# Gated delta rule: chunk inverses kept on the other half of the rows, products in four corners of the array

## The reference, cut to what matters

```python
lower = where(strict, einsum('bhnid,bhnjd->bhnij', kb, k) * decay, 0.0)   # kb = k * beta
tmat  = lower + eye(c)
sol   = triangular_solve(tmat, rhs, lower=True, unit_diagonal=True)
# then a scan over the chunks:
v_new = u_i - w_i @ state
o_i   = qg_i @ state + qk_i @ v_new
state = state * gl_i + kg_i^T @ v_new
```

## Time and profile before

| | |
|---|---|
| three runs | 1930.01, 1932.18 (median), 1933.41 us |
| the profiled execution | 1931.5 us; first to last instruction 1929.7 us |
| mean granted TensorE clock | 0.963 of full |
| PE busy, weight loads busy | 91%, 73% |
| DVE, ACT, POOL busy | 43%, 37%, 31% |
| stage A, B, C in this execution | about 1175 to 1199 us, 1199 to 1278 us, 1278 to 1288 us |

### The profile page before, as it was taken

The page is one execution under the profiler, slowest core; times in us unless marked ns, Lnnn a source line. Parts: engine busy times, 40 slices in busy tenths (PEclk is TensorE's granted clock), DMA queues, the critical chain, the costliest instruction groups (busy, mean ns, idle before and its releaser), DMA issues.

```text
span 1929.7 us, 32336 instructions
## 1 busy us (share of the span) xinstructions
PE 1747.3 (91%) x13588; PEld 1403.6 (73%) x13588; DVE 824.2 (43%) x1489; ACT 716.7 (37%) x1111; POOL 601.3 (31%) x318
## 2 busy tenths in 40 slices
PE   6799899978989988889889988888899899999996
PEld 2687788855878766667777757886578588888885
DVE  0301165447250255476547658655415433333112
ACT  3323413235342624354543965003434432222222
POOL 0121312183223323452024303212234234444442
PEclk9899999989999999999899999899999999999998
DMA  8344311130122211302432210000220223323231
GB/s 329 106 155 142 112 35 46 46 109 1 55 90 74 66 56 56 131 1 95 135 99 87 77 44 2 3 3 22 66 85 25 66 78 97 98 90 97 98 109 66
DMA packets 42569, 152.17 MB, mean 79 GB/s; under 512 B 4416, under 2 KB 5568, under 8 KB 42176
## 3 DMA queue, kind: packets, MB, share of 16 engines
q1 hardware_dynamic: 38880, 140.72, 22.1%
q10 hardware_dynamic: 3552, 9.44, 1.3%
HBM read 145.95 MB, written 4.19 MB: 78 GB/s over the span
## 4 chain that ended last, share of the span: by engine, by line
PE 41%; DVE 7%; ACT 2%; issue 2%; DVEq 0%; ACTq 0%
PE wide_ps L1770 29%; PE wide_ps L1791 2%; PE pair_ps L2344 1%; PE wide_ps L2341 1%; PE wide_ps L2320 1%; PE wide_ps L2279 1%; DVE xn L1688 1%; DVE xn L1538 1%; PE duo_ps L2448 1%; PE wide_ps L2429 1%; DVE h L1692 1%; PE wide_ps L1806 1%; DVE ring_r L1182 1%; PE pair_ps L2279 0%; DVE work L1598 0%
## 5 line engine op out<-in xcount | busy, mean ns | idle before, releaser
L534 POOL TENSOR_TENSOR ring_r<-ring,scratch_r 128x1024 fp32r<-128x1024 f32 x179 | 433.1, 2420 | 1075.9 <-ACT scratch_r L706 1047.8
L1770 PE MATMUL wide_ps<-xn_r,scratch_r 128*128 128x512 f32 (+1 forms) x1320 | 490.1, 371 | 0.0
L1770 PE MATMUL wide_ps<-work_r,scratch_r 128*128 128x512 f32 (+1 forms) x1151 | 445.9, 387 | 23.3 <-DVE xn_r L1174 12.4
L706 ACT ACTIVATE scratch_r<-ring 128x1024 fp32r<-128x1024 f32 x195 | 206.7, 1061 | 599.8 <-PE wide_ps L1770 457.4
L1770 PE MATMUL wide_ps<-work_r,ring_r 128*128 128x512 f32 (+1 forms) x1151 | 429.2, 373 | 0.0
L1770 PEld LDWEIGHTS wide_ps<-xn_r,scratch_r 128*128 128x128 f32 x1320 | 252.1, 191 | 49.3 <-issue 5.7
L1770 PEld LDWEIGHTS wide_ps<-work_r,scratch_r 128*128 128x128 f32 x1151 | 218.7, 190 | 75.7 <-issue 19.1
L1770 PEld LDWEIGHTS wide_ps<-work_r,ring_r 128*128 128x128 f32 x1151 | 218.9, 190 | 40.0
L1770 PE MATMUL wide_ps<-proj_r,scratch_r 128*128 128x512 f32 x704 | 238.1, 386 | 1.6 <-DVE proj_r L1174 1.6
L1770 PEld LDWEIGHTS wide_ps<-proj_r,scratch_r 128*128 128x128 f32 x704 | 132.8, 189 | 31.6 <-DVE proj_r L1174 2.5
L693 ACT ACTIVATE proj<-wide_ps 128x512 f32<-128x512 f32 (+2 forms) x116 | 73.9, 637 | 164.4 <-PE wide_ps L1770 154.8
(11 more groups left out here) (406 smaller groups left out, 2913.6 us busy)
## 6 DMA issues: line engine op xcount, KB each, us to landing
ring<-weights SPq DMA_DIRECT2D x256, 512.0 KB, 3.5
h<-tokens SPq DMA_DIRECT2D x4, 768.0 KB, 11.6
h<-tokens ACTq DMA_DIRECT2D x1, 3072.0 KB, 10.2
out<-h ACTq DMA_DIRECT2D x1, 2048.0 KB, 7.3
h<-out ACTq DMA_DIRECT2D x1, 2048.0 KB, 10.7
out<-h SPq DMA_DIRECT2D x8, 256.0 KB, 2.0
const_sb<-const SPq DMA_DIRECT2D x1, 1089.0 KB, 6.1
h<-mem ACTq DMA_DIRECT2D x1, 1024.0 KB, 13.2
```

What stands on the lines that cost most here:

```text
L534: pool.tensor_tensor(as_r(wt), wt, as_r(w_lead(m)).bitcast(F32), ALU.subtract).then_inc(w_split, 1)
L706: act.activation(as_r(w_lead(m)), ring[:, c % RING, :], ACT.Copy).then_inc(w_lead_ready, 1)
L1770: last = pe.matmul(wide_ps[:, bank, a:b], wt[:, cols], as_r(x[:, a:b]), start=n == 0 and p == 0, stop=n == len(k_order) - 1 and p == 2)
```

## The change

1. At level 0, `inverse_products` transposes `dn_inv_t` into the other half of the partitions, and ACT copies the result out (4 copies of 128x512, semaphore `dn_t0`); DVE's eight L1609 operations are gone.
2. The two 64-row L1598 operations of a step become one of 128 rows, with a stacked identity `idents` that is added to the constants.
3. `dn_inv` and `dn_half` live on the other half of the partitions for levels 1 to 5. `half_products` and the first kind of `inverse_products` go from a half of the rows to the other half of the columns, the second kind stays straight. No matmul is added or taken away.
4. ACT instead of DVE copies keys and values in stage A.
5. In stage C the eight near-block operations stand ahead of the far ones (`near_corners`) and no longer behind a wait on the second product; the two corner products swap straight and crossed.

```diff
@@ ACT, stage A
+                act.wait_ge(dn_tok_ps, n + 1)
+                act.activation(k_tok_2(c), by_head(dn_bank(6)), ACT.Copy)
+                act.activation(v_tok_2(c), by_head(dn_bank(7)), ACT.Copy).then_inc(dn_tok, 1)
+            for q in range(4):
+                act.wait_ge(dn_z_ps, q + 1)
+                act.activation(dn_inv(q), dn_bank(4 + q % 2), ACT.Copy).then_inc(dn_t0, 1)
@@ DVE, stage A
-                dve.wait_ge(dn_tok_ps, n + 1)
-                dve.tensor_copy(k_tok_2(c), by_head(dn_bank(6)))
-                dve.tensor_copy(v_tok_2(c), by_head(dn_bank(7))).then_inc(dn_tok, 1)
@@ DVE, half_masked
                 if 2 <= q < 6:
-                    dve.wait_ge(dn_t, q - 1)
-                dve.tensor_tensor(to_8(dn_half(p)), to_8(dn_bank(p % 2)), mask, ALU.mult).then_inc(dn_y, 1)
+                    dve.wait_ge(dn_y, q - 1)
+                masked = dve.tensor_tensor(to_8(dn_half(p)), to_8(dn_bank(p % 2)), mask, ALU.mult)
                 if l == 0:
...
-                    for r, rows in enumerate(HALF):
-                        dve.tensor_tensor(to_8(dn_inv_t(p))[rows], ident_8[r], to_8(dn_half(p))[rows], ALU.subtract)
+                    masked = dve.tensor_tensor(to_8(dn_inv_t(p)), idents_8, to_8(dn_half(p)), ALU.subtract)
+                masked.then_inc(dn_y, 1)
@@ DVE, order
             for q in range(steps + 1):
                 if q < steps:
                     half_masked(q)
-                if q:
+                if q > 4:
                     inverse_update(q - 1)
+            dve.wait_ge(dn_t, steps - 4)
+            for n in range(2):
+                near_corners(n)
             for n in range(2):
                 corners(n)
@@ PE, half_products
-                        last = pe.matmul(dn_bank(p % 2)[rows, HD * m:HD * m + HD], x, inv_t, start=True, stop=True, skip_group_check=True)
+                        to = HALF[1 - r] if l else rows
+                        last = pe.matmul(dn_bank(p % 2)[to, HD * m:HD * m + HD], x, inv_t, start=True, stop=True, skip_group_check=True)
@@ PE, inverse_products
-                        pe.matmul(halves(dn_bank(2 + p % 2)[rows, at], 1 << l)[:, :, side, :], dn_inv(p)[rows, at],
+                        pe.matmul(halves(dn_bank(2 + p % 2)[HALF[1 - r], at], 1 << l)[:, :, side, :], dn_inv(p)[rows, at],
```

More of the change, by code:

```diff
@@ L107 @@
 CONST2_COLS, N_CONST2 = table([("tri0", P), ("tri1", P), ("inv0", (LEVELS - 1) * HD), ("inv1", (LEVELS - 1) * HD),
-                               ("window", 3 * P), ("rot_half", P), ("inv_freq", 1)])
+                               ("window", 3 * P), ("rot_half", P), ("inv_freq", 1), ("idents", HD)])
 PAR_COLS, N_PAR = table([("c", 2 * KT), ("norm_g", DEPTH * KT), ("b_mod", DEPTH * N_MOD), ("conv_w", DEPTH * 6),
@@ L415, in q_grow, with inverse_done @@
             return by_head((cos_2, sin_2, conv_tmp[:, 0:LAT])[c - 1])
+        def inverse_done(engine, q):
+            engine.wait_ge(*((dn_t0, q) if q <= 4 else (dn_t, q - 4)))
         def dn_bank(n):
@@ L465, in build @@
         dn_y_ps, dn_y, dn_z_ps, dn_t = (sem(n) for n in ("dn_y_ps", "dn_y", "dn_z_ps", "dn_t"))
+        dn_t0 = sem("dn_t0")
         dn_p_ps, dn_p, dn_c_ps, dn_c, dn_r = (sem(n) for n in ("dn_p_ps", "dn_p", "dn_c_ps", "dn_c", "dn_r"))
@@ L1575, in lower_and_products @@
                     dve.tensor_tensor(dn_qk(u), kq, e, ALU.mult).then_inc(dn_x, 1)
-                dve.wait_ge(dn_tok_ps, n + 1)
-                dve.tensor_copy(k_tok_2(c), by_head(dn_bank(6)))
-                dve.tensor_copy(v_tok_2(c), by_head(dn_bank(7))).then_inc(dn_tok, 1)
-            ident_8 = [cst["ident"][rows, rows].unsqueeze(1).broadcast_to([HD, 8, HD]) for rows in HALF]
+            idents_8 = cst2["idents"].unsqueeze(1).broadcast_to([P, 8, HD])
             def half_masked(q):
@@ L1605, in inverse_update, with near_corners @@
                 dve.wait_ge(dn_z_ps, q + 1)
[L1606 to L1614, removed]
+                mine, other_side = (lambda v: halves(v, 1 << l)[:, :, side, :]), (lambda v: halves(v, 1 << l)[:, :, 1 - side, :])
+                dve.tensor_tensor(mine(dn_inv_t(p)), mine(dn_inv_t(p)), mine(dn_bank(2 + p % 2)), ALU.subtract)
+                dve.tensor_tensor(other_side(dn_inv(p)), other_side(dn_inv(p)), other_side(dn_bank(4 + p % 2)),
+                                  ALU.subtract).then_inc(dn_t, 1)
+            def near_corners(n):
+                for s in (2 * n, 2 * n + 1):
+                    for d in range(2):
+                        u, lo = dn_unit(d, s), HALF[0]
+                        factor = beta[:, chunk_at(d, s), 4 * d:4 * d + 4].unsqueeze(2).broadcast_to([P, 4, HD])
+                        dve.tensor_tensor(dn_lower(u)[lo, :, lo], by_head2(dn_inv_t(u // 2), s)[lo], factor[lo], ALU.mult)
             def corners(n):
@@ L1621, in corners @@
                         u, c = dn_unit(d, s), chunk_at(d, s)
-                        lo, to = HALF[0], HALF[d]
+                        to = HALF[d]
                         factor = beta[:, c, 4 * d:4 * d + 4].unsqueeze(2).broadcast_to([P, 4, HD])
-                        dve.tensor_tensor(dn_lower(u)[lo, :, lo], by_head2(dn_inv_t(u // 2), s)[lo], factor[lo], ALU.mult)
                         dve.tensor_tensor(dn_lower(u)[to, :, HALF[1 - d]], by_head2(dn_bank(n), s)[to], factor[to], ALU.mult).then_inc(dn_c, 1)
@@ L2312, in half_products @@
                 else:
-                    pe.wait_ge(dn_t, q - 3)
+                    inverse_done(pe, q - 3)
                 if q >= 2:
@@ L2316, in half_products @@
                 for m in range(8):
-                    for rows in HALF:
+                    for r, rows in enumerate(HALF):
                         x = dn_lower(2 * p + m // 4)[rows, m % 4, rows]
                         inv_t = dn_inv_t(p)[rows, HD * m:HD * m + HD] if l else cst["ident"][rows, rows]
-                        last = pe.matmul(dn_bank(p % 2)[rows, HD * m:HD * m + HD], x, inv_t, start=True, stop=True, skip_group_check=True)
+                        to = HALF[1 - r] if l else rows
+                        last = pe.matmul(dn_bank(p % 2)[to, HD * m:HD * m + HD], x, inv_t, start=True, stop=True, skip_group_check=True)
                 last.then_inc(dn_y_ps, 1)
@@ L2331, in inverse_products @@
                 if q >= 2:
-                    pe.wait_ge(dn_t, q - 1)
+                    inverse_done(pe, q - 1)
                 for m in range(8):
@@ L2335, in inverse_products @@
                     if l == 0:
-                        for rows in HALF:
-                            last = pe.matmul(dn_bank(4 + p % 2)[rows, at], dn_half(p)[rows, at], cst["ident"][rows, rows], start=True,
+                        for r, rows in enumerate(HALF):
+                            last = pe.matmul(dn_bank(4 + p % 2)[HALF[1 - r], at], dn_inv_t(p)[rows, at], cst["ident"][rows, rows], start=True,
                                              stop=True, skip_group_check=True)
                         continue
-                    for rows in HALF:
-                        pe.matmul(halves(dn_bank(2 + p % 2)[rows, at], 1 << l)[:, :, side, :], dn_inv(p)[rows, at],
+                    for r, rows in enumerate(HALF):
+                        pe.matmul(halves(dn_bank(2 + p % 2)[HALF[1 - r], at], 1 << l)[:, :, side, :], dn_inv(p)[rows, at],
                                   halves(dn_half(p)[rows, at], 1 << l)[:, :, side, :], start=True, stop=True, skip_group_check=True)
@@ L2355, in _ @@
             for n in range(2):
-                pe.wait_ge(dn_t, steps - 2 + 2 * n)
+                inverse_done(pe, steps - 2 + 2 * n)
                 for m in range(8):
@@ L2359, in _ @@
                         frm, to, p = HALF[1 - d], HALF[d], 2 * n + d
-                        last = pe.matmul(dn_bank(6 + n)[to, HD * m:HD * m + HD], dn_lower(2 * p + m // 4)[frm, m % 4, to],
+                        last = pe.matmul(dn_bank(6 + n)[frm, HD * m:HD * m + HD], dn_lower(2 * p + m // 4)[frm, m % 4, to],
                                          dn_inv_t(p)[frm, HD * m:HD * m + HD], start=True, stop=True, skip_group_check=True)
@@ L2366, in _ @@
                     for d in range(2):
-                        to, p = HALF[d], 2 * n + d
-                        last = pe.matmul(dn_bank(n)[to, HD * m:HD * m + HD], dn_inv(p)[to, HD * m:HD * m + HD],
-                                         dn_corner(n)[to, HD * m:HD * m + HD], start=True, stop=True, skip_group_check=True)
+                        frm, to, p = HALF[1 - d], HALF[d], 2 * n + d
+                        last = pe.matmul(dn_bank(n)[to, HD * m:HD * m + HD], dn_inv(p)[frm, HD * m:HD * m + HD],
+                                         dn_corner(n)[frm, HD * m:HD * m + HD], start=True, stop=True, skip_group_check=True)
                 last.then_inc(dn_c_ps, 1)
@@ L2573, in constants @@
                         + [np.where(t >= s, 0, NEG), np.zeros((P, P)), np.where(t <= s, 0, NEG), rotation(halves),
```

(2 more changed lines are left out.)

2 lines of the change are left out of this document (1 added, 1 removed).

## The result

| | median us | runs | from–to |
|---|---|---|---|
| before | 1930.01 | 5 | 1925.16–1933.41 |
| changed | 1916.33 | 5 | 1912.68–1919.89 |

The ratio is 0.9931 (95% interval 0.9904 to 0.9957), so the change brings 13.7 us, somewhere between 8 and 19. The forecast was 28.8 us (1903.4) with 1916 as the top of its range. The sign was right and the size about half; 1916.33 lies just above the range. The profiled execution of the changed kernel took 1912.68 us, its span is 1910.9.

A forecast was written before the change was run, and what follows sets the result against it. DVE was taken to bound level 0 of the inverses, PE levels 1 to 5. Gains of 8.1 + 18.6 + 2.1 = 28.8 us off 1932.18 gave 1903.4 us, range 1896 to 1916.

The forecast's parts named there:

- (a): Up to the start of `half_products(5)`: fewer DVE copies and shorter DVE steps at level 0; gain 8.1 us (6 to 10).
- (b): From `half_products(5)` to DVE's last update: four corners cut a step from 2.80 to 1.87 us; gain 18.6 us (15 to 25).
- Pauses and clock: Steps of levels 1 to 5: pauses of 0.25 us a step (0 to 0.5), plus 2 us lost to half clock (0 to 5).
- the very sign that the prediction names for its being wrong: Steps of levels 1 to 5: the forecast is wrong if pauses come to more than 0.5 us a step.
- 33.7 + 3.8: From `half_products(5)` to the last update: 18 steps of 1.87 us make 33.7 us, draining the last step 3.8 us.
- Rival 1: Inverse steps stay near 2.8 us: crossed and straight pairs hinder each other, or instructions can't come faster; 1918 us, chance 0.16.
- (c): Stage C: the eight near-block operations run during DVE's wait of 2.29 us; gain 2.1 us (0 to 2.3).
- Rivals 2 and 3: Inverse steps: 2, a 25 ns floor between records, 1914 us, chance 0.08; 3, array drains each turn, 1973 us, chance 0.03.

The follow-up runs named there:

- m1: Changed kernel plus 64 by 64 matmuls that wait for nothing behind PE's last work, written out and in loops, on four or two corners; 2032.18 us.
- e5: Changed kernel with PE's levels 1 to 5 as a loop of five turns, four corners, all 64 columns computed; 1903.96 us, ratio 0.9866.
- e1: Changed kernel with every product back on two corners, its other changes kept; 1914.25 us, ratio 0.9919.
- e4: Changed kernel with PE's levels 1 to 5 as a loop of five turns, on two corners instead of four; 1919.21 us, ratio 0.9946.

## Why the prediction was half right

**(a) 8.1 forecast, 6.6 measured.** Right in kind. The first masking came 1.6 us sooner, as forecast. The 128-row operation on DVE takes 1.04 us at best and 1.75 at worst, where I took 1.31. What I left out is a wait of DVE for PE:
```profile
1202.38 0.69 DVE L1601 TENSOR_TENSOR proj<-wide_ps,proj 128x512 f32<-128x512 f32 x1 [1.75 <-PE wide_ps L2334]
```
Level 0 is no longer DVE's alone. With 2 us a step for DVE, PE at half clock (0.61 from 1196 to 1204 us) is late once.

**(b) 18.6 forecast, 6.8 measured.** The step that failed is the paragraph "Pauses and clock", the term 18 x 0.25 = 4.5 us. The corners' rate (15 ns), the step without pauses (1.87 us) and DVE's ability to follow were all right. The pauses cost 2.84 − 1.87 = 0.97 us a step, four times the 0.25 I took and twice its upper bound, the very sign that the prediction names for its being wrong. With it the term is 18 x 0.97 = 17.5 us instead of 4.5, and 33.7 + 3.8 + 17.5 = 55.0 us, which is H5 to E as measured (55.35, 54.66). The cause is the supply of instructions, to which the prediction gave no limit in its sum. I bounded a pause by the one in rows 5 and counted one per step; what it shows is the remainder of a delivery that nearly keeps pace. The trace of before had the question in it, if not the answer: 13 blocks in 53 us is one block of 256 instructions per 4.1 us, and the new step asks for 192 instructions in 1.87 us, a block per 2.5 us. Nowhere in that trace do two packets of the instruction queue start less than 3.58 us apart. That the rate can't be exceeded was shown only by m1. L1889's 48 records couldn't tell, being fewer than the 128 of a block. Rival 1's last sentence named this cause, with a total of 1918 us, with too low a chance: its 0.16 was shared with a bank or row conflict. Its number was good; the reason it gives first, corners that hinder each other, is refuted by m1, e5 and the unpaused steps.

That (b) gained 6.8 all the same is mostly the clock (5.0), for which I had left a loss of 2 us in the new kernel. Low clock cost the kernel before 5 us over three steps (13.40 against 8.37 in e1); this gain was in rival 1 ("some 4 us"). The 2 us for the new kernel's own low clock were nearly nothing: from H8 to 1220 us the first trace of the changed kernel has a clock of 0.60, the second 1.00 in that place, and H8 to E takes 47.3 and 47.1 us. Where the supply was the limit anyway, the slower array cost next to nothing.

The Trainium skill (Runtime: NRT & Kernel Launch, Instruction fetch mechanics) says that PE's instruction stream is refilled in blocks of 16 KiB, 256 instructions, and that the cost of crossing a block's edge is mostly hidden. The block is what the trace shows. "Mostly hidden" holds for the two-corner stream (0.32 us in 27 us) and fails for four corners, where a crossing costs 1.38 to 1.93 us in m1.

**(c) 2.1 forecast, 3.6 measured**, of which stage C is 1278.15 to 1288.13 = 10.0 us before, 1263.01 to 1270.59 = 7.6 after: 2.4. The other part is the start of the scan. From the first multiplication to the next group of updates (L1644, after L1657) it took 7.15 us before (1288.16 to 1295.31) and 5.58 after (1270.62 to 1276.20). The granted clock of the first five microseconds tells why:
```profile
1288.00:1293.00 5.00, 4.09 (x22) 4.09 (x23) 2.56 (x5) 1.19 (x2) 0.00 (x0) 0.66 0.01 3
```
```profile
1270.60:1275.60 5.00, 4.24 (x38) 4.24 (x39) 3.73 (x6) 1.19 (x2) 1.33 (x3) 1.00 0.02 3
```
(before, then after). Before, PE had been idle for 5.44 us ahead of the scan; after, for 1.79. The first scan product that starts later fills that idle time. It repeats: the seven traces with the near blocks first have 5.58 or 5.59 us and a clock of 1.00 over these five microseconds, the four others 7.14 to 7.95 us and 0.50 to 0.66. I had mentioned the later start only as something to be covered.

**Rivals 2 and 3.** No floor of 25 ns: 128 records in 2.09 us. By the 25 ns that the Trainium skill states (TensorE: Matmul & The Clock Gate, Wait — 56ns, not 53.3ns?) they would have needed 3.2 us, an estimate from the page's figure; the measurement decides. And no drain at a turn: unpaused steps with 16 turns take 1.87 us.

**Does the forecast hold without the supply limit?** (a) and (b) together asked for 76.6 us from A to E (103.28 − 8.1 − 18.6). e5, with the pauses gone from four of five turns, has 77.1. That it fits so well is in part luck: A to H5 is 35.2 us where 32.5 were forecast, with a wait ahead of the loop among them, and H5 to E 41.9 where 44.0 were. So is its median of 1903.96 us beside the forecast of 1903.4: it is 25.9 us under that of the kernel before in the same comparison (1929.85), not 28.8.

## What to carry to other kernels

Count instructions, not only matmuls: written out, PE was fed 256 instructions per 3.5 to 4 us, so a speed-up of small matmuls below 27 to 31 ns for each pair of weight load and matmul record was lost. The sign is "issue" pauses at a steady distance, with packets of the instruction queue at the same distance and no engine full. When two limits lie at the same rate, removing one shows nothing; remove both together, as in the table of e1, e4 and e5. Where the body fits (768 instructions of products did, 1024 in m1), a loop on PE alone, with the other engines written out as they were, lifts the supply limit at some 0.35 us a turn. It pays only where the array is faster than the supply: with two corners (e4) it cost 2 us from A to E.

## What the runs showed of the hardware that I had not expected

- The supply of instructions is seen in the DMA view as its own queue: blocks of 16 KB, 256 instructions, in a steady stream at best one per 3.47 us (m1). What sets this time was not tested.
- A loop of 1024 PE instructions is delivered once and then runs from what is stored, at 15 ns a record.
- Four corners take one float32 record of 64 by 64 per 15 ns over 1640 records in a row, with PE's granted clock at 1.00.
- The low clock behind level 0 came back in a second execution (13.40 and 13.42 us for three steps), and each half of the change alone shortens it.
- At the start of the scan PE's granted clock was 1.00 behind 1.79 us of idle time in seven traces, and 0.50 to 0.66 behind 5.4 to 5.5 us in four.
